# A hybrid encoder step on one core: the scores of the next stick-breaking unit put ahead of the values of the present one, and the high parts of its sums rounded by the scalar engine

## What is computed

```python
def stick_breaking(q, k, v, q_pos, k_pos):
    z = jnp.einsum('bqhd,bkhd->bhqk', q, k) * (HEAD_DIM ** -0.5)
    mask = k_pos[None, :] < q_pos[:, None]
    log_1m = jnp.where(mask, jax.nn.log_sigmoid(-z), 0.0)
    tail = lax.cumsum(log_1m, axis=log_1m.ndim - 1, reverse=True) - log_1m
    a = jnp.where(mask, jnp.exp(jax.nn.log_sigmoid(z) + tail), 0.0)
    return jnp.einsum('bhqk,bkhd->bqhd', a, v)
```

## Time and profile before

| | us |
|---|---|
| median of 3 runs | 826.74 (826.5 to 828.31) |
| the profiled execution | 826.33 |
| its span in the profile | 824.5 |
| PE busy | 813.7 |
| DVE busy | 618.9 |
| ACT busy | 388.1 |
| POOL busy | 295.2 |

### The profile page before, as it was taken

The page is one execution under the profiler, slowest core; times in us unless marked ns, Lnnn a source line. Parts: engine busy times, 40 slices in busy tenths (PEclk is TensorE's granted clock), DMA queues, the critical chain, the costliest instruction groups (busy, mean ns, idle before and its releaser), DMA issues.

```text
span 824.5 us, 15910 instructions
## 1 busy us (share of the span) xinstructions
PE 813.7 (99%) x6154; PEld 798.6 (97%) x6154; DVE 618.9 (75%) x1073; ACT 388.1 (47%) x668; POOL 295.2 (36%) x213
## 2 busy tenths in 40 slices
PE   9999999999999999999999999999999999999996
PEld 7999999999999999999999999999999999999995
DVE  4687876356879999876338988488966889488996
ACT  5657775244667758544342333233332333323532
POOL 2562222225545545344434300651035300552330
PEclk9999999999999999999999999999999999999999
DMA  9653112451112211143313113531134113412203
GB/s 285 240 165 99 52 52 66 153 166 52 53 53 87 65 51 51 51 169 125 103 55 100 52 52 104 153 102 53 51 107 147 51 51 102 147 57 78 75 2 115
DMA packets 68416, 78.16 MB, mean 95 GB/s; under 512 B 2536, under 2 KB 65040, under 8 KB 67984
## 3 DMA queue, kind: packets, MB, share of 16 engines
q1 hardware_dynamic: 68080, 76.92, 28.9%
q10 hardware_dynamic: 288, 0.60, 0.2%
HBM read 70.15 MB, written 8.93 MB: 96 GB/s over the span
## 4 chain that ended last, share of the span: by engine, by line
PE 91%; DVE 6%; issue 1%; ACT 1%; DMA 1%; DVEq 0%; SPq 0%; ACTq 0%
PE pan L1560 59%; PE pan L1775 12%; PE att L1775 11%; PE att L1713 1%; PE att L1686 1%; PE pan L1616 1%; PE att L1703 1%; PE att L1560 1%; DVE xT L1393 1%; DMA x_rows<-in_x_sample 1%; PE att L1855 1%; PE pan L1646 1%; DVE sq_sum L1492 0%; PE att L1742 0%; DVE x_out L1479 0%
## 5 line engine op out<-in xcount | busy, mean ns | idle before, releaser
L473 POOL TENSOR_TENSOR w_lo<-raw,w_hi 128x512 fp32r<-128x512 f32 x160 | 222.8, 1416 | 416.0 <-ACT w_hi L813 178.4
L1560 PE MATMUL pan<-a_hi,w_hi 128*128 128x288 f32 x624 | 134.0, 296 | 0.0
L1560 PE MATMUL pan<-a_lo,w_hi 128*128 128x288 f32 x624 | 133.4, 295 | 0.0
L1560 PE MATMUL pan<-a_hi,w_lo 128*128 128x288 f32 x624 | 132.8, 294 | 0.0
L1560 PE MATMUL pan<-h_lo,w_hi 128*128 128x288 f32 x512 | 109.5, 296 | 0.0
L1560 PE MATMUL pan<-h_hi,w_hi 128*128 128x288 f32 x512 | 109.4, 295 | 0.0
L1560 PE MATMUL pan<-h_hi,w_lo 128*128 128x288 f32 x512 | 108.8, 294 | 0.0
L1560 PEld LDWEIGHTS pan<-a_hi,w_hi 128*128 128x128 f32 x624 | 99.7, 188 | 1.0
L1560 PEld LDWEIGHTS pan<-a_hi,w_lo 128*128 128x128 f32 x624 | 100.0, 188 | 0.0
L1560 PEld LDWEIGHTS pan<-a_lo,w_hi 128*128 128x128 f32 x624 | 99.5, 188 | 0.0
L1775 PE MATMUL pan<-F_hi,w_hi 128*128 128x288 f32 x320 | 95.4, 298 | 0.6 <-DVE xT L1393 0.6
(11 more groups left out here) (279 smaller groups left out, 1750.5 us busy)
## 6 DMA issues: line engine op xcount, KB each, us to landing
raw<-in_w_in SPq DMA_DIRECT2D x34, 512.0 KB, 4.8
raw<-in_w_up SPq DMA_DIRECT2D x32, 512.0 KB, 4.5
raw<-in_w_down SPq DMA_DIRECT2D x32, 512.0 KB, 4.7
raw<-in_w_out SPq DMA_DIRECT2D x8, 512.0 KB, 4.1
x_spill<-xT SPq DMA_DIRECT2D x1, 2304.0 KB, 7.0
xT<-x_spill SPq DMA_DIRECT2D x1, 2304.0 KB, 10.4
x_rows<-in_x_prompt SPq DMA_DIRECT2D x4, 512.0 KB, 6.8
raw<-in_w_pa SPq DMA_DIRECT2D x4, 512.0 KB, 4.4
```

The source lines that it names most:

```text
L473: last = nc.gpsimd.tensor_tensor(w_lo[:, slot, k:k + 4, :], raw[:, rs, k:k + 4, j * P:(j + 1) * P], w_hi[:, slot, k:k + 4, :].bitcast(F32) ...
L1560: got = nc.tensor.matmul(out[:, h, 0:HALF], w, x[:, h * HALF:(h + 1) * HALF], start=first and n == 0, stop=last and n == 2)
```

## The change

Three things are changed in the eight units.

1. TensorE does the scores of the next unit ahead of the values of the present one (`prompt_unit`). The scores write into the three banks that the present unit's weights are read from, so each bank now waits for `a_hi_ready` of the present unit, that is, for both Exp of that bank (`bank_free`). The first unit's scores stand ahead of the loop, the loop has three rounds, and the last pair is written out.
2. The high part of the sums is made by ACT (`sum_high`, a Copy) and no longer by DVE. ACT's list for the logs is now Exp B, Exp C, Ln B, Exp A, Ln C, copy B, Ln A, copy C, copy A (`prompt_logs`); each copy waits for DVE's add of its bank. On DVE the difference of bank B stands behind the add of C, that of C behind the add of A (`prompt_sums`).
3. The output of unit u'-1 is taken in unit u': by ACT behind Ln B (`take_out`), by DVE behind the add of B (`take_ob`, before behind the magnitudes).

```diff
+            def sum_high(u, n):
+                cs = slice(BANK[PROMPT_ORDER[n]], BANK[PROMPT_ORDER[n]] + PROMPT_W[PROMPT_ORDER[n]])
+                act.wait_ge(sp_added, u * 3 + (n + 3))
+                nc.scalar.activation(sp_hi[:, cs], sp[:, cs], ACT.Copy).then_inc(sp_hi_ready, 1)
+            def prompt_logs(u, out=None):
+                for n, bank in enumerate(PROMPT_ORDER):
+                    cs = slice(BANK[bank], BANK[bank] + PROMPT_W[bank])
+                    act.wait_ge(nabs_ready, u * 3 + n + 1)
+                    nc.scalar.activation(sp[:, cs], sp[:, cs], ACT.Exp).then_inc(e_ready, 1)
+                    if n:
+                        ln(u, n - 1, PROMPT_ORDER, PROMPT_W)
+                    if n == 1 and out:
+                        out()
+                sum_high(u, 0)
+                ln(u, 2, PROMPT_ORDER, PROMPT_W)
+                sum_high(u, 1)
+                sum_high(u, 2)
...
+            def take_out(i, q):
+                act.wait_ge(sbo_out, i * 2 + (3 + q))
+                own = slice(q * HD, (q + 1) * HD)
+                nc.scalar.activation(ob_hi[own, i, 0:SEQ], att[0:HD, 3, :], ACT.Copy).then_inc(sbo_hi, 1)
+                nc.scalar.activation(ob_lo[own, i, 0:SEQ], att[HD:P, 3, :], ACT.Copy).then_inc(ob_low, 1)
...
-                    sb_logs(u, PROMPT_ORDER, PROMPT_W)
+                    prompt_logs(u, out=(lambda: take_out(i, 0)) if q else (lambda: take_out(i - 1, 1)) if with_gates else None)
...
+            def prompt_sums(u, out=None):
+                sb_add(u, 0, PROMPT_ORDER, PROMPT_W, PROMPT_ADDS, 0)
+                if out:
+                    out()
+                sb_add(u, 1, PROMPT_ORDER, PROMPT_W, PROMPT_ADDS, 1)
+                sum_low(u, 0)
+                sb_add(u, 2, PROMPT_ORDER, PROMPT_W, PROMPT_ADDS, 2)
+                sum_low(u, 1)
+                sum_low(u, 2)
...
+            def prompt_unit(i, q, more=True):
...
+                panel(number + 1, slot4(2 * q + 1), 1, a_hi, a_lo, part=(6, KT))
+                if more:
+                    pe.wait_ge(kq_ready, i * 2 + (q + 2))
+                    prompt_scores(1 - q, free=i * 6 + 3 * q)
+                pe.wait_ge(sbo_taken, u)
+                pe.wait_ge(v_ready, i + 1)
+                for n, kbs in enumerate(((2, 3), (1,), (0,))):
+                    pe.wait_ge(a_split, i * 6 + (3 * q + n + 1))
```

More of the change, by code:

```diff
@@ L778, in sb_pair @@
                         stage_high(i + 1, q)
[L779 to L782, removed]
             sb_pair(0, with_gates=False)
@@ L787, in _ @@
             sb_pair(3, stage=False)
+            take_out(3, 1)
             sigmoids(3)
@@ L1154, in sb_split, with sum_low @@
                 nc.vector.tensor_tensor(sp_lo[:, cs], sp[:, cs], sp_hi[:, cs].bitcast(F32), ALU.subtract).then_inc(sp_split, 1)
[L1156 to L1161, removed]
+            def sum_low(u, n):
+                cs = slice(BANK[PROMPT_ORDER[n]], BANK[PROMPT_ORDER[n]] + PROMPT_W[PROMPT_ORDER[n]])
+                dve.wait_ge(sp_hi_ready, u * 3 + (n + 1))
+                nc.vector.tensor_tensor(sp_lo[:, cs], sp[:, cs], sp_hi[:, cs].bitcast(F32), ALU.subtract).then_inc(sp_split, 1)
+            def prompt_sums(u, out=None):
[7 more added lines that the diff above has]
+                sum_low(u, 2)
             for u in range(2):
@@ L1223, in _ @@
                     magnitudes(u, PROMPT_ORDER, PROMPT_W)
-                    if w:
-                        take_ob((w - 1) // 2, (w - 1) % 2)
-                    sb_sums(u, PROMPT_ORDER, PROMPT_W, PROMPT_ADDS)
+                    prompt_sums(u, out=(lambda: take_ob((w - 1) // 2, (w - 1) % 2)) if w else None)
                     if q:
@@ L1860, in _, with prompt_scores @@
                     sample_values(u)
-            def prompt_scores(q):
+            def prompt_scores(q, free=None):
                 def qk(kb, out, q0, start=False, stop=False):
@@ L1866, in qk, with bank_free @@
                     return acc(out, k_st[q][:, kb * P:(kb + 1) * P], q_lo[q][:, q0:SEQ], stop=stop)
+                def bank_free(n):
+                    if free is not None:
+                        pe.wait_ge(a_hi_ready, free + n)
                 strict = mask2[:, P:2 * P]
+                bank_free(1)
                 acc(att[:, 1, 0:P], ident_b[:], strict, start=True)
                 acc(att[:, 1, 256:384], ident_b[:], strict)
+                bank_free(2)
                 acc(att[:, 2, 0:P], ident_b[:], strict, start=True)
-                acc(att[:, 0, 0:P], ident_b[:], strict, start=True)
@@ L1873, in prompt_scores @@
                 qk(2, att[:, 1, 0:256], 256)
                 qk(3, att[:, 1, 256:384], 384, stop=True).then_inc(z_out, 1)
+                bank_free(3)
+                acc(att[:, 0, 0:P], ident_b[:], strict, start=True)
                 qk(1, att[:, 2, 0:384], 128, stop=True).then_inc(z_out, 1)
                 qk(0, att[:, 0, :], 0, stop=True).then_inc(z_out, 1)
+            def prompt_unit(i, q, more=True):
+                u = i * 2 + (2 + q)
+                number = first_panel(i + 5) + 2 * q
+                panel(number, slot4(2 * q), 0, a_hi, a_lo)
+                panel(number + 1, slot4(2 * q + 1), 1, a_hi, a_lo, part=(0, 4))
+                tails(u, PROMPT_ORDER, prompt_tails,
+                      before_last=lambda: panel(number + 1, slot4(2 * q + 1), 1, a_hi, a_lo, part=(4, 6)))
+                panel(number + 1, slot4(2 * q + 1), 1, a_hi, a_lo, part=(6, KT))
[6 more added lines that the diff above has]
+                    pe.wait_ge(a_split, i * 6 + (3 * q + n + 1))
+                    for kb in kbs:
+                        _, c, q0, w = PROMPT_KB[kb]
+                        v = v_st[:, kb, q].rearrange("p a n -> p (a n)")
+                        acc(att[:, 3, q0:SEQ], v, sp_hi[:, c:c + w], start=kb == 2)
+                        got = acc(att[:, 3, q0:SEQ], v, sp_lo[:, c:c + w], stop=kb == 0)
+                got.then_inc(sbo_out, 1)
@@ L1878, in _ @@
             pe.wait_ge(tile_taken, 44)
-            with pe.Fori(0, 4) as i:
+            pe.wait_ge(kq_ready, 1)
+            pe.wait_ge(a_ready, 6)
+            prompt_scores(0)
+            with pe.Fori(0, 3) as i:
                 for q in range(2):
[L1881 to L1901, removed]
@@ L1903, in _ @@
+                    prompt_unit(i, q)
+            prompt_unit(3, 0)
+            prompt_unit(3, 1, more=False)
             pe.wait_ge(sbo_taken, 8)
```

## The result

| | before | the change |
|---|---|---|
| median, us | 827.02 (826.5 to 828.31, 4 runs) | 837.48 (835.77 to 838.68, 4 runs) |
| the profiled execution | 826.33 | 835.77 |
| its span | 824.5 | 834.0 |

The ratio is 1.0123, with an interval of 1.0101 to 1.0144: 10.5 us slower. That was the direction forecast and, as the rows show, most of it comes by the mechanism forecast; the time lies 1 us above the upper end of the range.

A forecast was written before the change was run, and what follows sets the result against it. PE bounds the kernel, busy 813.7 of 824.5 us, so only its waits in the eight units count. 826.33 - 1.5 + 6.0 + 0.6 + 0.8 = 832.2, taken as 832.4; 8 in 10 range 827.0 to 836.5.

The forecast's parts named there:

- The values' waits: In seven units the values' last bank no longer waits 0.22 us for DVE's `a_split`: -1.5 us.
- The chain of ACT: Unit 2: copy A, then loads and sigmoids of 5.0 us to 257.7; PE's three masks at 258.6, 259.4, 260.35.
- 2.0 us a gate unit, three of them: +6.0: Next unit's scores wait for banks freed by ACT's late weights in units 2, 4 and 6: +6.0 us.
- tails of C in even units: Sign that the prediction is wrong: PE idle at such places, which it did not expect; no size given.
- unit 3 0.76 for 0.6: Unit 3's tails wait for DVE's difference of C: 1.0 with all collisions, none without, taken as 0.6 us.
- unit 5 1.77 for 1.9: Unit 5's tails wait 1.9 us, after two gate products on DVE, in place of 1.09: +0.8.
- The tails also come 1.26 us later, which gives the logs and sums more time: In each unit the values now lie between scores and tails, giving ACT's logs and DVE's sums 1.26 us more.
- Rival C: Faster: unit 2's chain is short enough, no scores wait, both old waits go; 823.9 us; chance 0.07.
- Collisions with POOL: Unit 2's DVE steps keep four long instructions inside POOL's run; without any collision they take 2.4 us less.
- Rival B: DVE and POOL collide half the time, add A ends near 251, wait 0.8 or less a gate unit; 827; chance 0.13.
- The load: Gate units' table load costs its 1.28 us and nothing behind it, against the Trainium skill's 1.38 us of drain.
- and nothing behind it: The span from 206 to 350 us grows by about 6, and nothing later in the kernel grows.

The follow-up runs named there:

- the first experiment: Kernel before with only TensorE's list of the change (scores ahead of values, bank waits), ACT's and DVE's lists untouched: 826.97 us, ratio 0.9987.
- sigmoids between the copies: The change with gate units' loads and sigmoids moved from behind ACT's copies to between Ln A and copy A: 827.74 us, ratio 1.0001.
- a further move: DVE's gate products moved behind the sums, on scores ahead alone (825.42 us, ratio 0.9972) and with sigmoids between the copies (825.43 us, ratio 0.9974).
- the experiment: The change with two further table loads behind the sigmoids of each gate unit: 846.38 us, ratio 1.0225.
- the execution of 837.67 us: The change run again unaltered, for the profile alone: 837.67 us, span 835.9.
- the other repeat: The change run again unaltered, for the profile alone: 835.36 us, span 833.5.
- the copies alone: The change with TensorE's old order (values first, no `bank_free`), keeping ACT's and DVE's new lists: 841.41 us, ratio 1.0164.
- no loads: The change with the sigmoids of gate units 2, 4 and 6 replaced by same-size copies and their two table loads left out: 828.12 us, ratio 1.0007.

## Why the time came out above the range

**The values' waits: right.** The pitch of an unhindered unit is 17.58 us, 0.21 less than before, and the first experiment shows it alone.

**The chain of ACT: right to 0.1 us, the wait sized 0.3 too small.** The first Exp of unit 2 was forecast for 257.7 and stands at 257.61; the three masks were forecast for 258.6, 259.4 and 260.35 and stand at 258.54, 259.31 and 260.29. What was off is when PE would have been there. The sum had PE want its scores at 257.6 and, without waits, come to the mask of A at 258.35. But the values' wait is saved in this unit too: by the pitch of 17.58, PE was ready for its scores at 257.35 (239.77 and 17.58), while DVE's and ACT's chain took as long as before. So unit 2 costs 2.31, not 2.0: a wait saved ahead of a place that waits anyway is given back there.

**The step that failed in the units: unit 2 stood for all gate units, "2.0 us a gate unit, three of them: +6.0".** Units 4 and 6 have a product of gates on DVE ahead of the magnitudes, unit 2 has none. In unit 4 of the change, on DVE, ACT and PE:

```profile
279.40 1.49 DVE L1239 TENSOR_TENSOR m_a<-m_a,gate 128x576 f32<-128x576 f32 x1
280.81 1.61 DVE L1156 TENSOR_SCALAR sp<-att 128x384 int32<-128x384 int32 x3
...
290.88 0.63 ACT L695 ACTIVATE sp_hi<-sp 128x512 fp32r<-128x512 f32 x1 [2.23 <-DVE sp L1169]
...
291.50 0.45 PE L1807 MATMUL att<-sp_hi,suffix 128*128 128x384 f32 x1 [0.38 <-DVE sp_lo L1184]
```

The magnitudes begin 2.80 us after the scores (at 278.01), in unit 2 1.39 (241.16 and 239.77), and copy A 12.87 us after them, in unit 2 12.18. Of these 0.69 us PE pays 0.55 at the tail of C and 0.14 at the banks. The forecast had 2.0 and no tail wait in each of these units; they cost 3.0 each. With the gate products moved on the change itself, the tail wait is gone and copy A stands at 12.36 (290.33 less 277.97). The prediction named "tails of C in even units" as a sign that it is wrong, and the sign is there.

**The sum of these.** Bank waits 7.2 for 6.0, tails of units 4 and 6 1.1 for 0, unit 3 0.76 for 0.6, unit 5 1.77 for 1.9: 8.2 us in place of 5.9. That alone gives 834.5 for the profiled execution, inside the range; what carried the time past its end comes last in this section.

**"The tails also come 1.26 us later, which gives the logs and sums more time": fell.** The first experiment has the tail wait of unit 5 at 0.89 us where it was 0.64 before. DVE works there without a gap, so it is its list that is full, and the time given lies where DVE has other work. Rival C counted 1.1 us for this wait. Neither kernel without bank waits (scores ahead alone, sigmoids between the copies) loses it, and they took 826.97 and 827.74 where C had 823.9; 825.4 took a further move.

**Collisions with POOL: near enough.** The sum kept four long instructions on DVE; in the row they are 1.02, 1.03, 0.82 and 1.54, together 4.41 where the forecast had 0.69, 1.73, 0.42 and 1.53, together 4.37. The lengths were traded among the instructions. Those with both inputs in SBUF are the long ones, while the scalar_tensor_tensor, with an operand in PSUM, keeps 0.56 inside POOL's run. The Trainium skill (SBUF — State Buffer, SBUF: two separate sides) says that a DVE instruction with two inputs in SBUF and a GpSimd instruction that reads SBUF hold the shared ports in turn, each for its whole length; these rows agree. Rival B, which had the add of A end near 251, is out: it ended at 251.91.

**The load: the row was right.** The load costs 1.29 us to the next instruction (252.60 to 253.89), and each further load in the experiment cost 1.29. The 1.38 us of drain that the Trainium skill (ScalarE: Activation LUTs, What ACT_TABLE_LOAD costs) puts behind a load is not seen here.

**The step that failed behind the units: "and nothing behind it".** The profiled execution is 9.4 us above that of before: 8.2 are the units', and 1.2 are two rounds of a later loop that ran at a slower pace. In the execution of 837.67 us it is 8.2 for the units, 2.3 where the clock had fallen behind a bank wait, and 0.7 for a slower pace behind the units. The sum had both terms at nothing, and no row of before shows either. It also put the median 0.2 us above the profiled execution, and it lies 1.7 above. The three executions of the change that were timed with the profiled one have no trace. Their mean granted clock is 0.994, 0.994 and 0.993, like the 0.993 of the execution of 837.67 us and unlike the 0.998 of the profiled one, so the clock had probably fallen in them too; that is argued, not shown. So the 2.3 us by which the units were undersized and these two terms together put the median above the range; either alone would not have, as far as these numbers tell.

## What to carry to other kernels

An instruction that waits for another engine holds back its engine's whole list: what stands behind it can no longer be done during the wait. Before making one engine wait for a short result, list what is queued behind and who needs it. Here 5 us that had been free lay behind copy A, and putting them into ACT's idle time ahead of it gave back all of the loss.

When a pattern of units is costed from one unit, check which of the others has an extra instruction ahead of the chain. Give no later consumer credit for time unless the producer has a gap in which to use it. And a microsecond lost on the busiest engine is a microsecond of the kernel only if nothing behind it was going to wait anyway.

## What the runs showed of the hardware

**After a wait the clock falls in some executions and not in others.** Granted clock of TensorE (the column of 1.00) and matmuls (x, first pair of brackets) right behind the bank waits of unit 2, first in the profiled execution of the change:

```profile
258.00:261.50 3.50, 2.19 (x15) 1.78 (x16) 2.36 (x4) 3.50 (x8) 0.26 (x1) 1.00 0.00 0
261.50:264.50 3.00, 3.00 (x24) 2.91 (x23) 2.31 (x5) 2.96 (x6) 3.00 (x3) 1.00 0.00 0
```

And in the one that took 837.67 us:

```profile
258.00:261.50 3.50, 2.10 (x14) 1.70 (x15) 2.26 (x4) 3.50 (x8) 0.16 (x1) 0.98 0.00 0
261.50:264.50 3.00, 3.00 (x12) 2.81 (x12) 2.41 (x5) 2.96 (x6) 3.00 (x3) 0.50 0.00 0
264.50:267.50 3.00, 3.00 (x24) 3.00 (x23) 2.14 (x4) 2.98 (x7) 2.69 (x3) 0.96 0.00 0
```

The waits ahead are the same in both, 1.03, 0.48 and 0.29 us. In one the clock stays at 2.4 GHz, in the other it stands at half, 1.2 GHz, over the 3 us of the second row, half the matmuls are done, and the pitch is 21.48 instead of 19.89: 1.6 us. But not all of that reaches the end. DVE and ACT run on meanwhile, so unit 3's tails find their sums ready, and its pitch is 17.57 instead of 18.34: 0.8 us net. The clock fell again in unit 6 there (22.10 against 20.56), where nothing behind gives it back. In the other repeat it fell in unit 4 (22.13 against 21.15), and the waits of unit 5's tails went with it (17.79 against 18.78), so it cost nothing: from the first B tails to the last unit's values it is 139.17 us in that repeat and in the first profile alike, and 141.48 in the execution of 837.67 us.

With the two loads more the clock fell in all three gate units, and with the copies alone in two. In the profiles of kernels without such waits it never fell over the eight units. In the first profile of the change, and in that of the change with the gate products moved, it did not fall either, though both have the waits. What decides it is open.

**The pace of a loop without waits.** The down-projection's loop stands long behind the units. Each of its rounds runs at one of two paces, with the granted clock full in both. The chain that ended last, in order of time (start, us), in the change:

```profile
494.19 4.80 PE pan L1807 x36
...
589.95 4.72 PE pan L1807 x36
...
685.09 4.80 PE pan L1807 x36
```

That is 131.1 ns a matmul or 133.3, which makes 0.6 us a round of the loop. The first and third round are slow here, the first in one repeat, none in the other, and the third in two of the experiments (scores ahead alone, no loads). The kernel before, twice, and all others have none. The stretch of 624 matmuls between the units and this loop has two lengths as well, 82.2 us (the kernel before and the change among them) and 82.8 (the execution of 837.67 us and four of the experiments). Executions of one program differ in both, so the code alone does not set it, and its cause stays open. Differences of up to 1.2 us between two profiles of this kernel can be of this kind.
